# A decoder layer on one core: the down product of chunk 9 is computed plainly, and ScalarE and VectorE take other orders in the first FFN steps

## What is computed

```python
def rmsnorm(x, g):
    xf = x.astype(jnp.float32)
    y = xf * lax.rsqrt(jnp.mean(xf * xf, axis=-1, keepdims=True) + RMS_EPS)
    return (y * g.astype(jnp.float32)).astype(x.dtype)
...
        x = x + jnp.einsum('bse,ed->bsd', mixed, w_out)
        h = rmsnorm(x, ffn_norm)
        g = jnp.einsum('bsd,df->bsf', h, w_gate)
        u = jnp.einsum('bsd,df->bsf', h, w_up)
        x = x + jnp.einsum('bsf,fd->bsd', jax.nn.silu(g) * u, w_down)
    return rmsnorm(x, final_norm)
```

## Time and profile before

| | |
|---|---|
| median of three runs | 294.99 us |
| the profiled execution | 295.97 us |
| its span, first to last instruction | 294.1 us |
| TensorE matmul busy (PE) | 284.9 us, 97% of the span, 1396 instructions |
| VectorE busy (DVE) | 263.4 us, 90% |
| ScalarE busy (ACT) | 190.0 us, 65% |
| GpSimd busy (POOL) | 24.7 us, 8% |
| share of PE in the chain that ended last | 80% |
| granted TensorE clock, mean | 0.995 of full speed |

### The profile page before, as it was taken

The page is one execution under the profiler, slowest core; times in us unless marked ns, Lnnn a source line. Parts: engine busy times, 40 slices in busy tenths (PEclk is TensorE's granted clock), DMA queues, the critical chain, the costliest instruction groups (busy, mean ns, idle before and its releaser), DMA issues.

```text
span 294.1 us, 4124 instructions
## 1 busy us (share of the span) xinstructions
PE 284.9 (97%) x1396; PEld 231.8 (79%) x1396; DVE 263.4 (90%) x422; ACT 190.0 (65%) x323; POOL 24.7 (8%) x30
## 2 busy tenths in 40 slices
PE   8999999999999999999999999999999999999990
PEld 4778888888788788888877888888888888888880
DVE  3888999998898869798899999999999999987984
ACT  4877668755796529849566574748484857664624
POOL 0001000000122504300000000000000000000063
PEclk9999999999999999999999999999999999999997
DMA  7999617798868827695676678685748391313003
GB/s 247 381 421 380 214 40 230 217 291 248 240 192 193 313 95 264 196 300 183 176 288 213 255 220 315 198 338 157 308 121 344 96 356 52 143 36 144 2 0 143
DMA packets 29653, 62.87 MB, mean 214 GB/s; under 512 B 3648, under 2 KB 16960, under 8 KB 28224
## 3 DMA queue, kind: packets, MB, share of 16 engines
q1 hardware_dynamic: 27616, 61.04, 61.1%
q10 hardware_dynamic: 2016, 1.57, 1.7%
HBM read 55.72 MB, written 1.11 MB: 193 GB/s over the span
## 4 chain that ended last, share of the span: by engine, by line
PE 80%; DVE 5%; DMA 5%; ACT 3%; SPq 2%; issue 2%; POOL 1%; POOLq 0%; ACTq 0%
PE bank L596 26%; PE bank L598 25%; PE bank L597 25%; DMA room<-in_first 3%; DMA room<-room 2%; PE bank L673 2%; SPq L503 1%; PE bank L623 1%; PE bank L646 1%; SPq L474 1%; DVE o_lo L1439 1%; PE bank L606 1%; ACT x_hi L942 1%; ACT o_hi L1093 1%; POOL rot L1649 1%
## 5 line engine op out<-in xcount | busy, mean ns | idle before, releaser
L596 PE MATMUL bank<-w_hi,x_hi 128*128 128x512 f32 x224 | 88.9, 397 | 0.8 <-ACT room L1055 0.6
L598 PE MATMUL bank<-w_hi,x_lo 128*128 128x512 f32 x224 | 87.3, 390 | 0.0
L597 PE MATMUL bank<-w_lo,x_hi 128*128 128x512 f32 x224 | 87.3, 390 | 0.0
L596 PEld LDWEIGHTS bank<-w_hi,x_hi 128*128 128x128 f32 x224 | 42.1, 188 | 11.2 <-ACT room L1055 1.0
L598 PEld LDWEIGHTS bank<-w_hi,x_lo 128*128 128x128 f32 x224 | 42.0, 188 | 8.9
L597 PEld LDWEIGHTS bank<-w_lo,x_hi 128*128 128x128 f32 x224 | 42.1, 188 | 8.2
L910 ACT ACTIVATE w_hi<-raw 128x1024 fp32r<-128x1024 f32 x33 | 33.7, 1049 | 10.4 <-issue 9.9
L1217 DVE TENSOR_TENSOR w_lo<-raw,w_hi 128x1024 fp32r<-128x1024 f32 x32 | 38.3, 1211 | 1.8 <-ACT w_hi L910 1.7
L1376 DVE TENSOR_TENSOR w_lo<-raw,w_hi 128x1024 fp32r<-128x1024 f32 x30 | 36.2, 1217 | 1.2 <-ACT w_hi L1043 0.9
L1043 ACT ACTIVATE w_hi<-raw 128x1024 fp32r<-128x1024 f32 x29 | 30.2, 1052 | 0.0
L1054 ACT ACTIVATE rope_b<-bank,rstd 128x256 f32<-128x256 f32 x22 | 10.3, 470 | 28.5 <-PE bank L598 28.3
(11 more groups left out here) (151 smaller groups left out, 500.9 us busy)
## 6 DMA issues: line engine op xcount, KB each, us to landing
raw<-in_weights SPq DMA_DIRECT2D x74, 512.0 KB, 5.5
room<-in_weights SPq DMA_DIRECT2D x10, 1024.0 KB, 6.8
room<-room SPq DMA_DIRECT2D x76, 64.0 KB, 2.1
room<-in_first SPq DMA_DIRECT2D x1, 1024.0 KB, 8.4
xs<-in_x SPq DMA_DIRECT2D x2, 512.0 KB, 10.0
rot<-turned_sums SPq DMA_DIRECT2D x8, 128.0 KB, 3.9
room<-in_first SPq DMA_DIRECT2D x2, 384.0 KB, 5.1
room<-room ACTq DMA_DIRECT2D x12, 64.0 KB, 2.7
```

The source lines that it names most:

```text
L596: pe.matmul(dst, a_hi, w1, start=first, stop=False)
L597: pe.matmul(dst, a_hi, w2, start=False, stop=False)
L598: return pe.matmul(dst, a_lo, w1, start=False, stop=last)
```

## The change

Three things are changed.

1. **Chunk 9's down product is plain.** `LAST_FORMED` goes from 9 to 8: chunks 0 to 8 are computed by 7 products, chunk 9 by 8 products of blocks (`ninth`), chunk 10 as before (`tenth`). `hidden_sums`, `down_sums` and the parts of the sums fall away for chunk 9. `down_second(8)` moves ahead of the second half of `gate_up(10)`, and so the 7 banks are complete one half-step earlier; they are combined on VectorE between the splits of the last weights.
2. **The end of the right quarter.** TensorE adds the residual of the last 256 columns itself: ScalarE and VectorE split it into `end_x`, and two matmuls of 256 columns with a unit matrix (`unit_r`) bring it into the bank. ScalarE then takes the squares of this quarter straight from PSUM, and VectorE scales it from PSUM. The squares of the left quarter move to VectorE, the gain of quarters (0, 0) and (0, 1) moves from GpSimd to VectorE, that of (1, 0) from VectorE to GpSimd, and GpSimd adds up three sums of squares instead of taking one from VectorE.
3. **Other orders in steps 0 to 3**, on ScalarE and VectorE. TensorE's order there stays as it is.

```diff
-LAST_FORMED = NCH - 2
+LAST_FORMED = NCH - 3
...
@@ tensor, last_downs @@
+                def ninth(dst, s, n, cols, first=True):
+                    for t in range(FT):
+                        plain(dst, 1, UNITS_AT[s, t], more_hi, more_lo, BLOCK_AT[t, n], cols, first and t == 0, False)
...
+                pe.wait_ge(lo_ready, STEP1_PAIR + (NCH - 1) * G_PAIRS + 2)
+                pe.wait_ge(ht_lo, 2 * LAST_FORMED + 3)
+                ninth(bank[PRODUCT_BANK[4]], 0, 0, whole, False)
+                pe.wait_ge(combined, 3)
+                ninth(bank[PRODUCT_BANK[6]], 0, 1, whole)
                 turn_last_hidden()
+                ninth(bank[PRODUCT_BANK[2]], 1, 0, whole, False)
+                ninth(bank[PRODUCT_BANK[3]], 1, 1, left)
+                pe.wait_ge(end_lo, 1)
+                pe.wait_ge(end_hi, 2)
+                pe.matmul(bank[PRODUCT_BANK[1]][:, right], unit_r, end_x[0], start=True, stop=False)
+                pe.matmul(bank[PRODUCT_BANK[1]][:, right], unit_r, end_x[1], start=False, stop=False)
+                ninth(bank[PRODUCT_BANK[1]], 1, 1, right, False)
+                pe.wait_ge(lo_ready, STEP1_PAIR + (NCH - 1) * G_PAIRS + 4)
                 pe.wait_ge(last_lo, 1)
+                tenth(bank[PRODUCT_BANK[4]], 0, 0, whole)
+                tenth(bank[PRODUCT_BANK[6]], 0, 1, whole)
+                tenth(bank[PRODUCT_BANK[2]], 1, 0, whole)
+                tenth(bank[PRODUCT_BANK[3]], 1, 1, left)
+                tenth(bank[PRODUCT_BANK[1]], 1, 1, right)
@@ tensor, step @@
                 down_first(c - 2)
+                if c == NCH - 1:
+                    down_second(c - 2)
                 pe.wait_ge(evacuated, 2 * c + 1)
                 for h in range(2):
                     gate_up_half(c, 1, h)
-                down_second(c - 2)
+                if c < NCH - 1:
+                    down_second(c - 2)
@@ scalar, steps 0 to 2 @@
             evacuate(0, 0)
+            gate_up_hi(2, 0)
             evacuate(0, 1)
...
-            gate_up_hi(2, 0)
             gate_up_hi(2, 1)
             down_first_hi(0, 0)
             gate_up_hi(2, 2)
-            hidden_hi(0)
             gate_up_hi(2, 3)
             down_first_hi(0, 1)
+            hidden_hi(0)
...
             evacuate(2, 0)
+            down_second_hi(0)
             hidden_hi(1)
             hidden_sums_hi(1)
-            down_second_hi(0)
@@ scalar, step @@
+                gate_up_hi(c + 1, 1)
+                if c > 3:
+                    hidden_hi(c - 1)
                 else:
+                    evacuate(c, 0)
+                gate_up_hi(c + 1, 2)
+                if c > 3:
+                    evacuate(c, 0)
+                else:
+                    hidden_hi(c - 1)
+                hidden_sums_hi(c - 1)
+                gate_up_hi(c + 1, 3)
+                down_second_hi(c - 2)
+                evacuate(c, 1)
@@ scalar, end @@
+            act.wait_ge(end_done, 5)
+            sum_squares(bank[PRODUCT_BANK[1]][:, NH:NB], NH, ssq2[:, 9:10], MEAN_SCALE)
@@ vector, steps 0 to 3 @@
-            for s in range(SH):
-                multiply(0, s)
-                turn_squares(0, s)
+            multiply(0, 0)
+            turn_squares(0, 0)
             gate_up_lo(2, 0)
+            multiply(0, 1)
+            turn_squares(0, 1)
...
+            multiply(2, 0)
             hidden_sums(1)
-            multiply(2, 0)
+            down_second_lo(0)
             turn_squares(2, 0)
             hidden_lo(1)
-            down_second_lo(0)
...
-                hidden_sums(c - 1)
+                if c > 3:
+                    hidden_sums(c - 1)
                 gate_up_lo(c + 1, 2)
                 multiply(c, 0)
+                if c == 3:
+                    hidden_sums(c - 1)
@@ vector, last_step @@
+                hidden_lo(c - 1)
+                multiply(c, 0)
+                dve.wait_ge(p1_copied, 1)
+                dve.tensor_tensor(c11, p1, c11, ALU.add).then_inc(combined, 1)
...
+                ninth_down_lo(0)
...
+                dve.tensor_tensor(part_w, p7, part_u, ALU.add).then_inc(combined, 1)
+                dve.tensor_tensor(part_v, p5, part_u, ALU.add).then_inc(combined, 1)
+                dve.tensor_tensor(c22, p7, c22, ALU.add).then_inc(combined, 1)
+                ninth_down_lo(1)
...
@@ vector, end @@
+            add_end(1, 1, left, bank[PRODUCT_BANK[3]])
+            last, end_left = bank[PRODUCT_BANK[1]][:, right], xs[:, 1, NB:NB + NH]
+            dve.wait_ge(res_done, 12)
+            dve.tensor_tensor_reduce(out=normed[:, 1, 1, left], in0=end_left, in1=end_left, scale=1.0 / D_MODEL,
+                                     scalar=EPS, op0=ALU.mult, op1=ALU.add, accum_out=ms[:, 1:2]).then_inc(ms_end, 1)
...
@@ gpsimd, end @@
+            inverse_rms_of_parts((8, 9), 7, 8)
             pool.wait_ge(in_gout, 16)
...
+            pool.wait_ge(res_done, 11)
+            pool.tensor_tensor(normed[:, 1, 0, :], xs[:, 1, 0:NB], gain_out[:, 0:NB], ALU.mult).then_inc(gained_pool, 1)
+            pool.wait_ge(sq_done, 9)
+            pool.wait_ge(ms_end, 1)
+            link(pool.tensor_tensor(msq[:, 9:10], ssq[:, 9:10], ms[:, 1:2], ALU.add))
+            pool.wait_ge(sq_done, 10)
+            link(pool.tensor_tensor(msq[:, 9:10], msq[:, 9:10], ssq2[:, 9:10], ALU.add))
+            pool.tensor_tensor(rstd[:, 9:10], msq[:, 9:10], neg_half[:, 9:10], ALU.pow).then_inc(rstd_ready, 1)
```

More of the change, by code:

```diff
@@ L842, in last_downs @@
-                whole = slice(0, NB)
-                for s, n, to in ((0, 0, PRODUCT_BANK[4]), (0, 1, GU_BANK), (1, 0, PRODUCT_BANK[2])):
-                    for t in range(FT):
-                        ins = plain(bank[to], t, s, n, whole, to == GU_BANK and t == 0, t == FT - 1)
-                    ins.then_inc(end_done, 1)
-                for t in range(FT):
-                    ins = plain(bank[PRODUCT_BANK[3]], t, 1, 1, slice(0, NH), False, t == FT - 1)
-                ins.then_inc(end_done, 1)
@@ L850, in last_downs, with plain @@
-                pe.wait_ge(p1_copied, 1)
-                pe.wait_ge(combined, 5)
-                for t in range(FT):
-                    ins = plain(bank[PRODUCT_BANK[1]], t, 1, 1, slice(NH, NB), t == 0, t == FT - 1)
-                ins.then_inc(end_done, 1)
+                def plain(dst, h, x, hi, lo, j, cols, first, last):
+                    return three_products(dst[:, cols], h_hi[:, h, x, :], h_lo[:, h, x, :], hi[:, j, cols], lo[:, j, cols],
+                                          first, last)
@@ new lines, in last_downs, with tenth @@
+                whole, left, right = slice(0, NB), slice(0, NH), slice(NH, NB)
+                def ninth(dst, s, n, cols, first=True):
+                    for t in range(FT):
+                        plain(dst, 1, UNITS_AT[s, t], more_hi, more_lo, BLOCK_AT[t, n], cols, first and t == 0, False)
+                def tenth(dst, s, n, cols):
+                    for t in range(FT):
+                        ins = plain(dst, 0, t * SH + s, down_hi, down_lo, 2 * t + n, cols, False, t == FT - 1)
+                    ins.then_inc(end_done, 1)
@@ L1167, in step @@
[L1167 to L1173 removed]
+                act.wait_ge(part_done, 1)
+                act.activation(part_p1, bank[PRODUCT_BANK[1]][:], ACT.Copy).then_inc(p1_copied, 1)
+                ninth_down_hi(0)
+                ninth_down_hi(1)
+                last_down_hi(0)
@@ L1574, in _ @@
-            dve.wait_ge(res_done, 13)
-            add_end(1, 1, right, 5, bank[PRODUCT_BANK[1]])
-            last = xs[:, 1, NB + NH:2 * NB]
-            dve.wait_ge(res_done, 14)
-            dve.wait_ge(ms_end, 1)
-            dve.tensor_tensor_reduce(out=normed[:, 1, 1, right], in0=last, in1=last, scale=1.0 / D_MODEL,
-                                     scalar=ms[:, 0:1], op0=ALU.mult, op1=ALU.add,
-                                     accum_out=ms[:, 1:2]).then_inc(ms_end, 1)
-            with_gain(1, 0, full, 11)
@@ new lines, in _ @@
+            dve.tensor_tensor_reduce(out=normed[:, 1, 1, left], in0=end_left, in1=end_left, scale=1.0 / D_MODEL,
+                                     scalar=EPS, op0=ALU.mult, op1=ALU.add, accum_out=ms[:, 1:2]).then_inc(ms_end, 1)
+            for cols, x in ((right, last), (left, end_left)):
+                dve.wait_ge(rstd_ready, rstd_count["final"] + 1)
+                dve.scalar_tensor_tensor(normed[:, 1, 1, cols], x, rstd[:, 9:10],
+                                         gain_out[:, NB + cols.start:NB + cols.stop], ALU.mult,
+                                         ALU.mult).then_inc(fin_dve, 1)
```

218 lines of the change are left out of this document (83 added, 135 removed).

## The result

| | before | after |
|---|---|---|
| median of runs (lowest to highest), us | 295.13 (294.31 to 295.48), 6 runs | 296.76 (296.58 to 297.19), 6 runs |
| ratio after / before, 95% | | 1.0057 (1.0043 to 1.0072) |
| profiled execution: its time, span, us | 295.97, 294.1 | 296.73, 294.9 |
| PE busy, matmuls | 284.9 us (97%), 1396 | 285.9 us (97%), 1407 |
| start of the second FFN turn, us | 114.21 | 114.44 |

The change makes the kernel slower by 1.63 us.

What follows compares the result with a forecast made beforehand. The prediction took PE, busy 97%, as the bound. It summed +1.00 (matmuls) - 0.35 (orders) - 0.10 (tail) = +0.55 us onto the median 294.99, giving 295.5 us, no change that can be told; range 293.8 to 296.6.

Steps and rivals of the forecast that it cites:

- What bounds the kernel: Whole kernel: PE, busy 97%, is the bound; only fewer matmuls, closed gaps or a shorter tail pay.
- PE's work, +1.00: Chunk 9 and the residual: 18 matmuls of 512 columns and 14 of 256 replace 21 of 512, +1.00 us.
- The first gap, gone: PE's wait at 147.51 for `down_second_lo(0)`: closed by moving chunk 0's combine forward, -0.80 us there.
- the second gap, moved: PE's wait at 158.53 for `evacuate(3, 0)` closes; PE then waits at `down_second(1)` for `down_second_lo(1)`, about 1.2 us.
- The orders' -0.35: Steps 0 to 3: all new orders together win 0.46 us less 0.11 for the restart, out of 1.62.
- the median of the runs lies 0.98 us below that execution, so I add it to the median: Final sum: +0.55 us was added to the median, 294.99 us, rather than to the profiled 295.97 us.
- the bounds were 0 and -1.62: Limits on the orders' effect: 0 if the chain is no earlier, -1.62 us if it isn't the limit.
- The tail, -0.10: After the last matmul: squares wait for GpSimd's gain multiplication, last issue at t0 + 3.78 against 3.88, -0.10 us.
- the open tail: Rival, tail: squares and gain multiplication don't hold each other, 0.54 us shorter than forecast, 295.0 us; chance 0.15.
- before `ninth(0, 0)`: Rival, last step: VectorE's split is held by GpSimd's combining, PE waits 0.5 us, 296.0 us; chance 0.12.
- the late landing of chunk 2's pieces: Rival, step 3: late DMAs hold `hidden_hi(2)`; at 7.0 us, +3.0 us in all, 298 us; chance 0.13.
- Both gaps are won back: Rival, FFN: `down_second_lo(1)` ready at 163.4, all 1.62 us won, 294.3 us, or 293.7 with open tail; chance 0.20.

Runs made afterwards that it cites:

- run 6: The changed kernel with `down_second` ahead of the fourth gate and up split in the later steps too, on ScalarE and VectorE; 295.67 us, ratio 1.0018 to before.
- run 8: The kernel before with the new orders of steps 0 to 3 and `down_second` ahead in all steps; 294.96 us, ratio 0.9994 to before.
- run 5: The changed kernel with `down_second(1)`'s combines moved ahead in step 3 on ScalarE and VectorE; 295.37 us, ratio 1.0016 to before.
- run 2: The kernel before with only the new orders of steps 0 to 3; 296.14 us, ratio 1.0026 to before.
- run 4: The changed kernel with the gain multiplication of quarter (1, 0) on VectorE, behind its squares, not GpSimd; 296.06 us, ratio 1.0024 to before.
- run 7: The changed kernel with `down_second` ahead in all steps and the gain multiplication of quarter (1, 0) on VectorE; 295.15 us, ratio 0.9994 to before.

## Why the prediction missed

**What bounds the kernel**: right. PE is the bound, and only matmuls, gaps and the tail counted. The tail has one more uneven distance, at 279.29 in before and 279.24 after: there four matmuls of 128x128 turn the last hidden block. It is in both kernels and changes nothing.

**PE's work, +1.00**: right. Runs 6 and 8 have the same orders up to the last steps and the same idle time to 0.01 us; run 6 has the second FFN turn at 114.30 and t0 at 286.92, and the distances differ by 172.62 - 171.62 = 1.00 us.

**The first gap, gone; the second gap, moved**: the mechanism was right. The chain was forecast from `evacuate(3, 0)` to PE with 9.15 us and has 9.20; the distance of starts should have been 164.58 - 163.42 + 0.227 = 1.39 us and is 1.47. Run 5 shows that it is this chain: with `down_second(1)` taken forward the gap goes.

**The orders' -0.35**: this is the step that failed, as a size. Its minuend was the 1.62 us of gaps in one execution of before. Against that execution the orders bring -0.26, near enough. But the step "the median of the runs lies 0.98 us below that execution, so I add it to the median" took the offset to be a constant of the whole execution, and it wasn't: it sat in the very gaps that the sum took away. In the three other executions they are 0.61 us in the mean ((0.47 + 0.81 + 0.54) / 3), in all four 0.86. So the orders trade 0.61 to 0.86 us for 1.36, a loss of 0.50 to 0.75 us in place of the gain of 0.35, and run 2 measures +0.74 (0.4 to 1.1). Of the forecast's error of 1.63 - 0.55 = 1.08 us this is 0.85 to 1.10. The offset itself was too large as well: it was taken from a median of three runs, 294.99 us; six runs have 295.13 and 32 have 295.40, 0.57 us below that execution.

The signs were there. The ScalarE work ahead of the first gap waited for a DMA, and the execution was 0.98 us above its median, about the size of that gap. That the orders win nothing stood in the range's upper end, but a loss by them did not, since the bounds were 0 and -1.62: nothing in the text gave a reason to exclude a positive value.

**The tail, -0.10**: right, -0.16. The squares were held as forecast (1.47 against about 1.5), ending 0.27 us after GpSimd in place of 0.4. Run 4 shows that GpSimd's operation is what holds them: without it they take 0.43 us, so they aren't slow by themselves. Its -0.73 us can't be set beside the 0.54 by which the open tail was forecast to be shorter, since that sum kept the multiplication in GpSimd's list. By the Trainium skill, page "SBUF — State Buffer", section "Who interferes with whom", the loser of the shared interface blocks for the whole instruction of the other. The traces agree that there is a block, and that it is gone when the GpSimd instruction is; the squares end 0.27 us behind it, less than their own 0.43, so not all of their length is left when the block ends.

**The rivals**: the tail was not open; no gap of chunk 0's combine or before `ninth(0, 0)` showed; the late landing of chunk 2's pieces did not come in either profiled execution of the changed kernel, but run 7 had one at chunk 6, at 0.42 us. "Both gaps are won back" is what run 5 does. It wins 1.2 us on the changed kernel, near the 1.62 - 0.35 = 1.27 between the two forecasts, but it ends 0.5 us above before (ratio 1.0016) and not 0.72 below it, for the same reason as above. The loss needed no rival's mechanism.

**Together**: +1.00 + 0.75 - 0.16 = +1.59 us, or +1.34 with the mean of all four executions; measured +1.63 (1.3 to 2.1). The first sum is closer, but the interval doesn't choose between them, and part of that agreement may be luck.

## What to carry to other kernels

A gap that hangs on a DMA's landing, even on one some 17 us ahead of it, can differ from execution to execution: before you book its end as a gain, profile two or three executions, and when the profiled one is slower than the median, suspect that the difference sits in just these gaps, and count them at less. To find the landing that counts, measure from the issue to the reader: when that time is the same in both executions, the delay is older. A reordering that closes such gaps and opens one made of compute trades a cost that is paid now and then for one that is paid every time. When an operation is moved forward, the combine that the bound engine needs next must go forward with it (run 5); and in this kernel an operation of GpSimd on two SBUF operands was best kept out of the last stretch (run 4), though it looked free.
